# A block of four projections run tile by tile, an order of a first block, and three moved steps in a two-layer block kernel

## The reference

```python
x = x + rms_norm(y, post_mix_norm); h = rms_norm(x, pre_ffn_norm)      # first bound
x = x + rms_norm(f, post_ffn_norm)                                     # second bound
h = rmsnorm(x, norm_mix); proj = h @ w_in                              # 1024 -> 9792 columns
q, k, v, z, xbc, dt_raw, gate_a, gate_b = split(proj)
xbc = silu(depthwise_conv_centred(xbc)); xs, B, C = split(xbc)         # 5 taps
y = ssd(xs, dt, A, B, C) forward + backward + d_skip * xs              # 4 chunks of 128, 32 heads
y = y * silu(z); y = group_rms(y) * norm_g
x = x + (sigmoid(gate_a) * (attn @ w_a) + sigmoid(gate_b) * (y @ w_s)) @ w_out
x = x + cross_attention(rmsnorm(x, norm_cross), rmsnorm(mem, norm_mem))
x = x + square(relu(rmsnorm(x, norm_ffn) @ w_up)) @ w_down
```

## Time and profile before

| | |
|---|---|
| median of the runs | 1909.21 us (1907.79 to 1911.33) |
| the profiled execution's own time | 1912.35 us |
| its span, first to last instruction | 1910.5 us |
| PE busy | 1851.9 us (97%) |
| DVE busy | 1059.3 us (55%) |
| ACT busy | 811.5 us (42%) |
| POOL busy | 229.7 us (12%) |
| mean granted clock of PE | 0.992 of full |
| HBM read and written | 191.37 MB, 12.71 MB |

### The profile page before, as it was taken

How to read it: one execution, slowest core, us unless ns; L and a number is a source line. 1 busy time by engine, 2 the same in 40 slices (tenths; PEclk the granted TensorE clock), 3 DMA queues, 4 the chain that set the end, 5 groups by cost and what they waited for, 6 DMA issues and landing times.

```text
span 1910.5 us, 24022 instructions
## 1 busy us (share of the span) xinstructions
PE 1851.9 (97%) x9314; PEld 1522.4 (80%) x9314; DVE 1059.3 (55%) x1875; ACT 811.5 (42%) x1598; POOL 229.7 (12%) x299
## 2 busy tenths in 40 slices
PE   7999999999998899999999999999999999999998
PEld 7778798888887777788777887777888987878786
DVE  5355642343336687887879845566545453333433
ACT  5345442331235465564646634444434442222232
POOL 1405000000000014133252330000110000000000
PEclk9999999999999899999999999999999999999999
DMA  7211333333332343443333453233344223222221
GB/s 233 78 56 58 91 120 101 88 99 110 98 89 89 101 139 122 122 121 133 122 122 121 122 190 108 78 99 132 111 146 142 66 67 120 89 89 88 89 89 66
DMA packets 128113, 205.65 MB, mean 108 GB/s; under 512 B 26352, under 2 KB 58288, under 8 KB 127360
## 3 DMA queue, kind: packets, MB, share of 16 engines
q1 hardware_dynamic: 118960, 167.09, 28.2%
q0 software_dynamic: 8464, 34.93, 5.2%
q10 hardware_dynamic: 576, 2.10, 0.3%
HBM read 191.37 MB, written 12.71 MB: 107 GB/s over the span
## 4 chain that ended last, share of the span: by engine, by line
PE 78%; DVE 13%; ACT 4%; issue 2%; POOL 2%; DMA 1%; DVEq 0%; SPq 0%; ACTq 0%
PE m L1922 12%; PE m L1924 12%; PE m L1923 12%; PE m L1933 9%; PE m L1935 9%; PE m L1934 9%; PE s L2067 4%; DVE lo L1248 3%; PE s L2300 2%; PE m L2045 2%; PE m L2047 2%; PE m L2046 2%; PE s L2280 1%; DVE X L1602 1%; DVE X L1591 1%
## 5 line engine op out<-in xcount | busy, mean ns | idle before, releaser
L1922 PE MATMUL m<-hH,hi 128*128 128x512 f32 (+1 forms) x1392 | 533.9, 384 | 15.6 <-DVE lo L1248 6.8
L1924 PE MATMUL m<-hH,lo 128*128 128x512 f32 (+1 forms) x1392 | 511.2, 367 | 0.0
L1923 PE MATMUL m<-hL,hi 128*128 128x512 f32 (+1 forms) x1392 | 510.3, 367 | 0.0
L1248 DVE TENSOR_TENSOR lo<-raw,hi 128x1024 fp32r<-128x1024 f32 x299 | 368.7, 1246 | 175.5 <-ACT hi L813 175.1
L813 ACT ACTIVATE hi<-raw 128x1024 fp32r<-128x1024 f32 x299 | 308.9, 1050 | 242.1 <-PE m L1935 136.0
L1922 PEld LDWEIGHTS m<-hH,hi 128*128 128x128 f32 x1392 | 264.5, 190 | 61.8 <-DVE lo L1248 7.3
L1924 PEld LDWEIGHTS m<-hH,lo 128*128 128x128 f32 x1392 | 264.0, 190 | 43.6
L1923 PEld LDWEIGHTS m<-hL,hi 128*128 128x128 f32 x1392 | 264.8, 190 | 39.9 <-issue 1.0
L1933 PE MATMUL m<-hi,hH 128*128 128x512 f32 (+1 forms) x320 | 135.5, 424 | 5.6 <-DVE X L1539 5.6
L1935 PE MATMUL m<-hi,hL 128*128 128x512 f32 (+1 forms) x320 | 124.0, 387 | 0.0
L1934 PE MATMUL m<-lo,hH 128*128 128x512 f32 (+1 forms) x320 | 123.3, 385 | 0.0
(11 more groups left out here) (311 smaller groups left out, 2868.3 us busy)
## 6 DMA issues: line engine op xcount, KB each, us to landing
raw<-in_w_in_dram SPq DMA_DIRECT2D x72, 512.0 KB, 3.6
raw<-in_w_down_dram SPq DMA_DIRECT2D x54, 512.0 KB, 3.8
hn<-scr_cs_dram POOLq DMA_DIRECT2D x32, 512.0 KB, 4.2
raw<-in_w_up_dram SPq DMA_DIRECT2D x32, 512.0 KB, 4.6
raw<-in_w_gate_dram SPq DMA_DIRECT2D x44, 256.0 KB, 2.9
raw<-in_w_up_dram SPq DMA_DIRECT2D x44, 256.0 KB, 3.3
raw<-in_w_in_dram SPq DMA_DIRECT2D x33, 256.0 KB, 3.0
raw<-in_w_out_dram SPq DMA_DIRECT2D x16, 512.0 KB, 3.8
```

The costliest lines, as they stand in the source:

```text
L1248: e.tensor_tensor(d, r, h.bitcast(F32), ALU.subtract).then_inc(s_lo, 1)
L1922: e.matmul(bank, wh[:, kk, c], h[:, k, q], start=k == 0, stop=False)
L1923: e.matmul(bank, wh[:, kk, c], l[:, k, q], start=False, stop=False)
L1924: x = e.matmul(bank, wl[:, kk, c], h[:, k, q], start=False, stop=k == kt - 1)
```

## The change

1. The z blocks become "tmt": token tile by token tile, all four units needed in the first four slots. Their tanh and gate of tile 3 come one slot later; those of tiles 0 to 2 stay in their slots, the copies out of PSUM come in slots 4, 8, 12, 16 of the block.
2. The second token half of bc0: banks 0 and 1 as before in two slots each, then banks 2 and 3 together, unit by unit, in slots 12 to 15. They end together at slot 15 (bank 2 two slots later than before), and the units are let go at 12, 13, 14, 15. Convolutions 2 to 4 come one slot later. By the planner xs0's third and fourth units (101 and 102) are rounded at slots 389 and 390, before at 391 and 392; DVE's rests follow one slot behind.
3. At both bounds the squares of the first half row (S0) of tiles 0 to 2 come one slot later, into the slot of the second half, and so behind the rounding of a turned tile.
4. States 8 to 11 come one slot earlier: X+40, 41, 45, 46.
5. xq's units are rounded at most 8 slots ahead: slots 824, 826, 828, 830, before 820, 824, 826, 828. The ffn norm's gain is loaded ahead of xo's first unit, before ahead of xq's.

By the planner also: ex's third unit is rounded three slots later, z's second unit three slots earlier.

```diff
-        add(f"z{j}", "tm", 4, "aaaa")
+        add(f"z{j}", "tmt", 4, "aaaa")
...
-    "hd": lambda u: (2 * u - 2, 14 + (u > 2)) if u else (8, 8)
+    "hd": lambda u: (2 * u - 2, 11 + u) if u else (8, 8)
...
-        s = -1 if j < 4 else max(free[j - NHL] + 1 if j >= NHL else 8, at[-1] + 1, first[j] - 14)
+        s = -1 if j < 4 else max(free[j - NHL] + 1 if j >= NHL else 8, at[-1] + 1, first[j] - (8 if BLK["xq"].u0 <= j < BLK["xo"].u0 else 14))
...
-    "hd": lambda i: 9 + 2 * i
+    "hd": lambda i: (9, 11, 15, 15)[i]
...
-        N_S0.append(base + 1), N_S1.append(base + 2), N_HN.append(base + 3 + late), N_TR.extend([turn, turn + 1])
+        N_S0.append(base + 1 + (t < 3)), N_S1.append(base + 2), N_HN.append(base + 3 + late), N_TR.extend([turn, turn + 1])
...
-CV_T[:8] = [X0[0] + s for s in (-6, -4, -1, 2, 5, 9, 13, 17)]
+CV_T[:8] = [X0[0] + s for s in (-6, -4, 0, 3, 6, 9, 13, 17)]
...
-ST_T = [x + s for x in X0 for s in (15, 16, 20, 21, 25, 26, 36, 37, 41, 42, 46, 47)]
+ST_T = [x + s for x in X0 for s in (15, 16, 20, 21, 25, 26, 36, 37, 40, 41, 45, 46)]
...
-ZT_AT = [when([FIN[BLK[f"z{j}"].e0 + t] + d for j in range(4) for t in range(4)]) for d in (2, 3)]
+ZT_AT = [when([s0(f"z{j}") + 12 + t + d + (t == 3) for j in range(4) for t in range(4)]) for d in (2, 3)]
...
-    before = [None, 5, 6, 26, 29, 36, 37, 104, 105, BLK["ws0"].u0, BLK["ws0"].u0 + 1, BLK["xq"].u0, BLK["up1"].u0]
+    before = [None, 5, 6, 26, 29, 36, 37, 104, 105, BLK["ws0"].u0, BLK["ws0"].u0 + 1, BLK["xo"].u0, BLK["up1"].u0]
...
-                    f = s % 8 // 2
-                    for u in (2 * (s % 2), 2 * (s % 2) + 1):
+                    for f, u in [(s // 2 - 4, 2 * (s % 2)), (s // 2 - 4, 2 * (s % 2) + 1)] if s < 12 else [(2, s - 12), (3, s - 12)]:
```

More of the change, by code:

```diff
@@ L159, in uses @@
     n = b.nu
-    at = {"half": lambda u: (2 * u, 8 + 2 * u + 1), "hx": lambda u: (2 * u, 8 + 2 * u + 1), "hd": lambda u: (2 * u - 2, 14 + (u > 2)) if u else (8, 8), "fm": lambda u: (4 * u, 4 * u + 3), "ffm": lambda u: (u, 12 + u),
+    at = {"half": lambda u: (2 * u, 8 + 2 * u + 1), "hx": lambda u: (2 * u, 8 + 2 * u + 1), "hd": lambda u: (2 * u - 2, 11 + u) if u else (8, 8), "fm": lambda u: (4 * u, 4 * u + 3), "ffm": lambda u: (u, 12 + u),
           "tm": lambda u: (4 * u, 4 * u + 3), "tmt": lambda u: (u, 3 * n + u),
@@ L220, in finishes @@
         n = b.nu
-        at = {"half": lambda i: 14 + i // 2, "hd": lambda i: 9 + 2 * i, "hx": lambda i: 8 * (i // 4) + 6 + i % 4 // 2, "fm": lambda i: 4 * n - 4 + i,
+        at = {"half": lambda i: 14 + i // 2, "hd": lambda i: (9, 11, 15, 15)[i], "hx": lambda i: 8 * (i // 4) + 6 + i % 4 // 2, "fm": lambda i: 4 * n - 4 + i,
               "ffm": lambda i: n * i + n - 1, "tm": lambda i: 4 * n - 4 + i, "tmt": lambda i: n * i + n - 1,
```

## The result

The changed kernel takes **1885.32 us** at the median of 4 runs (1884.41 to 1886.15), the kernel before 1910.27 us in the same comparison (4 runs, 1907.79 to 1911.59). The ratio is 0.9871, with a 95% interval of 0.9854 to 0.9888: 21 to 28 us less. The forecast was 1881.4 with a range of 1874 to 1892. On the scale of the profiled executions it was 1884.5, and the changed kernel's profiled execution took 1884.41.

A forecast was written before the change was run, and what follows sets the result against it. PE's queue was taken as the bound, busy 1851.9 of 1910.5 us. Terms 1.9 + 1.9 + 5.2 + 10.7 + 4.8 + 4.8 = 29.3, less 1.5, gave 27.8; from 1909.21 that makes 1881.4, range 1874 to 1892.

The forecast's parts named there:

- squares, gu0 and bc0: Squares one slot later, behind the rounding, shrink PE's gaps: 1.9 us at gu0 and 1.9 at bc0.
- bc0's order: Earlier xs0 units close the 6.82 gap and 2.2 of clock; some 5 us waits at slot 409 instead; gain 5.2.
- z by token tiles: Later bank claims in z remove 5.6 us of gaps and 5.1 of halved clock behind three of them; gain 10.7.
- states: States 8 to 11 one slot earlier put XW ahead of POOL's root and close PE's waits; gain 4.8 us.
- xq and the gain: At xv, later rounding and no gain load ahead remove PE's 3.08 gap and 1.7 of clock; gain 4.8 us.
- new small waits: New waits of a few tenths, since PE runs 4 us ahead of DVE at each z's start: 1.5 us lost.
- rival 2: Clock dips in z and at xv stay, the new gap may bring a longer one; 6.8 us off, 1888; chance 0.16.
- Rival 1: The bubble does not move: DVE and ACT keep up with xs0; adds 5.6 us, 1876; chance 0.12.
- rival 4: z's weights come late at z+2 and z+3, past 2.8 us of cover; 37 us lost, 1918; chance 0.04.
- rival 3: DVE becomes the bound, taking back z's dips, half the loops' gaps and all of bc0's part; 1895; chance 0.07.
- leaves little slack: 0.1 each: In the state groups, PE turns the scaled tile one slot later after the earlier states, costing 0.1 us each.
- The shared port: Moved XWs on POOL could stretch DVE's taps and rests: up to 6.4 us for PE, taken as nothing.

The follow-up runs named there:

- experiment 3: Changed kernel with the first-half squares one slot earlier again at both bounds, all four ahead of the rounding: 1890.88 us, ratio to before 0.9898.
- experiment 2: Changed kernel with bc0's second half bank by bank again and convolutions 2 to 4 in their old slots: 1889.66 us, ratio to before 0.9893.
- experiment 8: Changed kernel with the transposes of the second xs tile and ACT's copy into XS one slot earlier in j = 0: 1883.39 us, ratio to before 0.986.
- experiments 6 and 7: Against the changed kernel, one run each: only the gain's load back ahead of xq's first unit, 1884.76; only the early rounding of xq's units back, 1886.78.

## Why the prediction held, term by term

The sum was 27.8. The profiles lie 27.9 apart, the medians 24.95. The near hit is partly luck, since the profiled execution of before happened to have a dip behind each gap that the sum priced with one, and more dips than its repeat at 1905.59. What each term was worth, as the loss when it alone is undone:

| term | predicted | undone alone | what the rows say |
|---|---|---|---|
| squares, gu0 and bc0 | 3.8 | 5.6 | 1.8 + 1.2 + 0.5 us of waits |
| bc0's order | 5.2 | 4.3 | 6.8 closed, 1.8 grows to 4.5, 1.1 on the way |
| z by token tiles | 10.7 | 4.8 | 5.3 of gaps, no dips |
| states | 4.8 | 3.5 | 4.8 closed, 2.2 opened |
| xq and the gain | 4.8 | 2.2 | a gap of 1.7 to 3.1 |
| new small waits | -1.5 | inside the others | LOW 2.2, XS 1.0 |
| sum | 27.8 | 20.4 | 24.95 for all together |

Each number of the third column is a difference of two medians from different comparisons and uncertain by 2 to 3 us (their ratios' intervals are some 3 us to either side), so xq's 2.2 can't be told from 0 or from 4.8 by the times; its row does that.

**Squares.** At gu0 the step held to the tenth (2.18 to 0.35). At bc0 the size of 1.9 was near, but its place was wrong: it was said to come off the claim's row, which still shows 1.7. It came off the wait for the tile's rest and the scaled tile, named there only as "two gaps on the way". By the waits the term is 3.5 against 3.8; the 5.6 of the medians is within its uncertainty of that, and in the profiles the difference is where a dip fell and the first 35 us (experiment 3).

**bc0's order.** It held as laid out: by PE's position from bc0 to slot 409 it earned 10.5 - 5.5 = 5.0 against 5.2, the wait at slot 409 is 4.51 against "some 5", the loss on the way 1.10 against 1. PE's first state came at 674.97. The layout had put it 5.2 earlier than before; it came 10.5 earlier, of which 5.5 were earned upstream. The layout named no price for the clock behind the new wait, only that a longer dip could come (rival 2): it did, at some 2.5 us where the dip behind the wait of 1.82 had cost 1.7. Rival 1, that the bubble does not move, falls with that wait and with experiment 2. What the layout did not name is whose queue decides: "the ACT copy" was there as late next, but not that ACT could have made it 1.5 us earlier, which experiment 8 shows.

**z.** This is the step that failed in size. Its first half, 5.6 of gaps, measured 5.3. Its second half, 3 x 1.7 for the clock, is not owned by z: undone alone it brought no dip in two profiles, and no lower clock in the timed runs. The words "each of the three is followed by 1.7 us lost to the clock" were true of that one profile and were taken as a property of the gap. Rival 2 (the dips stay, 1888) did not come as it was told: the stretches of z and xv in the changed kernel are at full clock. But its doubt was the right one. The dips are no fixed cost of the gaps, and on average the kernel before pays less for them than the profile that was priced. The cover for the weights, 2.8 us, held: there is no wait for L1248, so rival 4, the one on the slower side, is out, and so is rival 3, with DVE busy 6.90 of 7 us around z1's claim as before and PE never waiting.

**States.** The closed waits came as forecast. The step "leaves little slack: 0.1 each" failed: it was 0.6 each, 2.2 in all. The tile was put at one slot later without asking how long the four operations behind it take:

```profile
845.31 1.67 DVE L1622 SCALAR_TENSOR_TENSOR LOW<-LOW,ST,gain 128x256 f32<-128x256 f32 x4
847.13 0.52 PE L2066 MATMUL s<-CST,LOW 128*128 128x128 f32 x3 [0.60 <-DVE LOW L1622]
```

**xq and the gain.** The mechanism held, and experiments 6 and 7 show that the change does it twice over. The 3.08 was one draw of a gap that three others put at 1.66 to 1.76.

**The shared port.** In the changed kernel two XWs take 2.67 us together at 673.71, beside DVE's L1595 and a rest of 1.63; in experiment 8 two take 1.65, and the mean of all 48 is 0.81 each. The Trainium skill (SBUF — State Buffer, Who interferes with whom) says that a DVE operation with two SBUF inputs and a GpSimd operation that reads SBUF exclude each other: one holds the shared ports for a whole instruction, the other waits. The rows agree that such operations stretch each other; that one waits for the whole of the other they don't show. Outside slot 409 it did not cost PE what it might have: with all sixteen XWs moved, none is waited for longer than 0.5. At slot 409 PE's matmul started 1.26 us behind the start of the first XW (674.97 - 673.71), where the shortest of the 48 takes 0.60, so up to 0.6 us may have gone there (an estimate from these two). Since POOL's durations in a profile are rough, the place of PE's next matmul, 674.97, is the firmer number.

**What is open.** 20.4 of the 24.95 are owned by single parts. The rest, 4.5, lies within the spread of those five differences. The clock has a share in the whole that can be read off: the changed kernel's four timed runs were granted 0.9968 in the mean (0.996 to 0.997), the 21 runs of the kernel before beside the experiments 0.9935 (0.992 to 0.995). The difference is 0.0033 of some 1900 us, so about 6 of the 24.95 are clock and 19 are gaps (an estimate; a dip that falls into a wait counts in it and costs nothing). Of the five kernels with one part undone only that with bc0's old order was granted clearly less than the changed one, 0.9953 in the mean, some 3 us. The other 3 us of clock are owned by no single part in these runs. Why dips get fewer with the gaps, and why the changed kernel's two stand where they do, is not shown.

## What to carry to other kernels

Price each gap of the engine that bounds by its own row, then lay the chain behind it out again with that engine out of the way, queue by queue: part of the gap comes back some slots later, and the last link there may be a different engine from the one that was busiest. A wait that is closed by moving work one slot opens at the next consumer of what was moved, unless that one has its own duration to spare. And look at a clock dip or a late transfer in several profiles before putting it into a sum as if it belonged to its gap. A dip that falls just ahead of a wait costs nothing there: the wait is shorter by as much.

## What was not expected of the hardware

- The same kernel with the same gaps drew different dips: in three profiles of before, the three stretches in z were at 0.89 in all three, in all three, and in one; times 1912.35, 1912.57 and 1905.59. The Trainium skill (TensorE: Matmul & The Clock Gate, Part 1) says that the chip judges the engine's activity on a cycle of its own, not tied to the kernel's start, so that one program has a different number of slow matmuls from run to run. These rows agree that the number differs, here in the middle of a kernel and behind gaps of 1.8 us; on what cycle the chip judges they don't show.
- A load of 512 KB behind the gain's landed so that the same wait was 3.08, 1.66, 1.75 and 1.76 us in four profiles: a price taken from a wait for DMA is good to a factor of two here.
- A dip can be free. With a dip just ahead, z0's claim in the kernel before waited 0.28 us and without one 1.90; the third wait for a scaled tile at bc0 was 0.86 with a dip just ahead (the changed kernel) and 2.36 without.
- DVE's rest of 128 x 1024 took 1.63 us beside POOL's XW (at 674.27 in the changed kernel) and 1.21 without it (at 671.37).
